# A hybrid trunk layer on one core: memory queries projected earlier, softmax work regrouped between ScalarE and VectorE, mixed scale from a ones matmul

## What is computed

```
h    = RMSNorm(x);  proj = h @ W_in          # q,k,v, gates, pooling input u, memory query q_m
gla  = chunked gated linear attention(q,k,v) , head RMSNorm, * silu(gate)
pool = multi-scale causal mean of u minus u, grouped linear, * silu(gate)
s    = q_m . k_mem / 8                       # 4 heads, 256 memory tokens
p    = softmax(s);  mem = (p . v_mem) * silu(gate)
mixed = concat(gla, pool, mem)
y    = RMSNorm(x + mixed @ W_out)
```

## Time and profile before

| | |
|---|---|
| Median of 3 runs | 1571.4 us (1571.22 to 1571.52) |
| The profiled execution | 1571.57 us, span 1570.1 us |
| TensorE busy | 1442.4 us, 92% of the span |
| VectorE, ScalarE, GpSimd busy | 746.9, 577.3, 334.9 us |
| Chain that ended last | 82% TensorE, 8% VectorE, 3% ScalarE, 2% GpSimd |
| Mean granted TensorE clock | 0.972 of full |

### The profile page before, as it was taken

How to read it: one execution, slowest core, us unless ns; L and a number is a source line. 1 busy time by engine, 2 the same in 40 slices (tenths; PEclk the granted TensorE clock), 3 DMA queues, 4 the chain that set the end, 5 groups by cost and what they waited for, 6 DMA issues and landing times.

```text
span 1570.1 us, 28228 instructions
## 1 busy us (share of the span) xinstructions
PE 1442.4 (92%) x11714; PEld 1042.9 (66%) x11714; DVE 746.9 (48%) x1221; ACT 577.3 (37%) x973; POOL 334.9 (21%) x298
## 2 busy tenths in 40 slices
PE   3259699999999999999999999999999999999985
PEld 2238576766768676776867576676867676676752
DVE  2775626455361726445262635436172645526162
ACT  1344424344342424334242434434242433424231
POOL 1321303031220303122221303122030313122110
PEclk9679799999999999999999999999999999999998
DMA  8130100101020010102010010102001010201001
GB/s 339 56 134 2 41 1 28 54 13 67 0 80 0 27 53 27 53 0 80 0 63 17 27 53 18 62 0 80 0 27 53 27 53 0 80 0 54 1 28 67
DMA packets 15432, 69.32 MB, mean 44 GB/s; under 512 B 2352, under 2 KB 2480, under 8 KB 12848
## 3 DMA queue, kind: packets, MB, share of 16 engines
q1 hardware_dynamic: 15408, 68.98, 11.9%
HBM read 52.20 MB, written 16.78 MB: 44 GB/s over the span
## 4 chain that ended last, share of the span: by engine, by line
PE 82%; DVE 8%; ACT 3%; issue 3%; POOL 2%; DMA 1%; SPq 1%; ACTq 0%; POOLq 0%; DVEq 0%
PE bank L330 69%; PE bank L467 2%; PE bank L475 2%; PE bank L481 2%; PE bank L489 2%; PE bank L532 1%; DVE whl L836 1%; DVE arena L979 1%; DVE nm L988 1%; DVE arena L997 1%; POOL arena L1156 1%; ACT arena L715 1%; PE bank L383 1%; DVE arena L962 1%; DVE mx L985 1%
## 5 line engine op out<-in xcount | busy, mean ns | idle before, releaser
L330 PE MATMUL bank<-arena,whl 128*128 128x256 f16 x6144 | 683.8, 274 | 3.0 <-DVE whl L836 3.0
L330 PEld LDWEIGHTS bank<-arena,whl 128*128 128x128 f16 x6144 | 601.6, 98 | 84.5 <-issue 7.0
L330 PE MATMUL bank<-arena 128*128 128x512 f16 x1536 | 343.5, 381 | 12.3 <-DVE arena L856 12.3
L330 PEld LDWEIGHTS bank<-arena 128*128 128x128 f16 x1536 | 148.2, 98 | 184.8 <-issue 18.6
L947 DVE SCALAR_TENSOR_TENSOR arena<-arena 64x256 f32<-64x256 f32 x60 | 25.2, 420 | 411.9 <-POOL arena L1173 410.5
L330 PE MATMUL bank<-whl,arena 128*128 128x512 f16 x768 | 168.4, 379 | 0.0
L676 ACT ACTIVATE arena<-bank,sca 128x512 f32<-128x512 f32 x64 | 43.9, 687 | 262.8 <-PE bank L330 261.7
L330 PEld LDWEIGHTS bank<-whl,arena 128*128 128x128 f16 x768 | 75.1, 98 | 87.3
L1156 POOL TENSOR_TENSOR arena<-arena 128x512 f16<-128x512 f32 x64 | 89.5, 1410 | 142.3 <-ACT arena L724 142.3
L1166 POOL TENSOR_TENSOR arena<-arena 128x542 f32<-128x542 f32 x16 | 17.3, 1079 | 463.9 <-issue 438.8
L867 DVE SCALAR_TENSOR_TENSOR arena<-bank,sca,arena 128x512 f32<-128x512 f32 x64 | 47.8, 749 | 108.0 <-PE bank L330 91.4
(11 more groups left out here) (154 smaller groups left out, 1516.0 us busy)
## 6 DMA issues: line engine op xcount, KB each, us to landing
arena<-in_xt SPq DMA_DIRECT2D x16, 1024.0 KB, 5.4
arena<-in_x SPq DMA_DIRECT2D x32, 512.0 KB, 3.4
out<-arena SPq DMA_DIRECT2D x32, 512.0 KB, 2.6
arena<-in_w_in SPq DMA_DIRECT2D x8, 768.0 KB, 16.1
arena<-in_w_out SPq DMA_DIRECT2D x1, 4096.0 KB, 12.2
arena<-in_w_in SPq DMA_DIRECT2D x8, 392.0 KB, 16.2
arena<-in_w_mem SPq DMA_DIRECT2D x1, 2048.0 KB, 10.9
arena<-in_memt SPq DMA_DIRECT2D x1, 1024.0 KB, 6.5
```

The costliest lines, as they stand in the source:

```text
L330: mm = nc.tensor.matmul(ap, lhs, rhs, start=k == 0 and n == 0, stop=(k, n) == last)
```

## The change

Five edits, all of them within a pass:

- The memory query is projected second of the four groups, into bank 1; the two gates follow in banks 2 and 3. ScalarE makes the high part of `qst` ahead of the last two gates, and the load of the exponential table now stands behind the last gate.
- VectorE takes the maxima of units 0 and 1 ahead of the masks; the scaled negative maximum `nm` is made by ScalarE.
- `p_norm` is only the reciprocal. The division happens within the split: ScalarE's high part and VectorE's new `p_low` read `pr` and multiply by the reciprocal, head by head (128 x 256 each).
- GpSimd no longer makes the rest of the probabilities.
- The all-reduce is gone: `mix_sum` on TensorE multiplies the per-partition maxima by a matrix of ones into bank 6, behind the keys of the next pass (and at the head of the tail). The scale then comes from the sum of the maxima. GpSimd's carry of S waits for the state and the head outputs.

```diff
+            def mix_sum(n):
+                pe.wait_ge(mmax_ok, n + 4)
+                nc.tensor.matmul(bank[6][:, 0:1], ones[:, :], mmax[:, 1:2], start=True, stop=True).then_inc(m_all, 1)
...
                 features(2, CK).then_inc(pe_k, 1)
+                if not first:
+                    mix_sum(i - 1)
...
-                for n, c in enumerate((CU, CGP, CGM, CQM)):
+                for n, c in enumerate((CU, CQM, CGP, CGM)):
...
-                    if n < 2:
+                    if n == 0:
+                        pe.wait_ge(p2_out, 5 * i + 4)
+                        pe.wait_ge(qm_lo, 2 * (i + 1))
+                    elif n == 1:
                         pe.wait_ge(p2_out, 5 * (i + 1))
-                        pe.wait_ge(qm_lo, 2 * (i + 1))
...
             def tail(n):
+                mix_sum(n - 1)
...
-                silu(4, 1, 4)
-                silu(5, 2, 6)
-                nc.scalar.preload_act_table_set(EXP_LN)
-                act.wait_ge(pe_p2, 6 * i + 6)
+                act.wait_ge(pe_p2, 6 * i + 4)
...
+                silu(5, 2, 4)
+                silu(6, 3, 6)
+                nc.scalar.preload_act_table_set(EXP_LN)
                 act.wait_ge(pe_ket, i + 1)
...
                 def p_exp_of(n):
+                    act.wait_ge(max_ok, 4 * i + n + 1)
+                    nc.scalar.activation(nm[:, 2 * n:2 * n + 2], mx[:, 2 * n:2 * n + 2], ACT.Copy,
+                                         scale=sc_neg).then_inc(nmax_ok, 1)
                     act.wait_ge(nmax_ok, 4 * i + n + 1)
...
-                    nc.scalar.activation(phl[n % 2][:, 0, :, :], pr[n % 2], ACT.Copy).then_inc(p_hi, 1)
+                    for h in range(2):
+                        a = nc.scalar.activation(phl[n % 2][:, 0, h, :], pr[n % 2][:, h, :], ACT.Copy,
+                                                 scale=rsum[:, 2 * n + h:2 * n + h + 1])
+                    a.then_inc(p_hi, 1)
...
-                nc.vector.tensor_scalar(m_tmp, mmax[:, 2:3], TINY, None, ALU.max).then_inc(m_tiny, 1)
+                nc.vector.tensor_scalar(m_tmp, bank[6][:, 0:1], TINY, None, ALU.max).then_inc(m_tiny, 1)
...
-                    r = rsum[:, 2 * n:2 * n + 2].unsqueeze(2).broadcast_to([P, 2, NMEM])
-                    nc.vector.tensor_tensor(pr[n % 2], pr[n % 2], r, ALU.mult).then_inc(pn_ok, 1)
+                def p_low(n):
+                    dve.wait_ge(p_hi, 4 * i + n + 1)
+                    for h in range(2):
+                        a = nc.vector.scalar_tensor_tensor(phl[n % 2][:, 1, h, :], pr[n % 2][:, h, :],
+                                                           rsum[:, 2 * n + h:2 * n + h + 1], phl[n % 2][:, 0, h, :],
+                                                           ALU.mult, ALU.subtract)
+                    a.then_inc(p_lo, 1)
...
-                for n in range(4):
-                    p_lo_of(i, n)
...
-                nc.gpsimd.partition_all_reduce(mmax[:, 2:3], mmax[:, 1:2], P, RMAX).then_inc(m_all, 1)
```

More of the change, by code:

```diff
@@ L692, in step @@
                     r = slice(64 * h, 64 * h + 64)
-                    nc.scalar.activation(qst[r, :, h, :], bank[3][r, :].rearrange("p (a t) -> p a t", a=2), ACT.Copy,
+                    nc.scalar.activation(qst[r, :, h, :], bank[1][r, :].rearrange("p (a t) -> p a t", a=2), ACT.Copy,
                                          scale=2.0 ** -QBITS).then_inc(qm_hi, 1)
+                silu(5, 2, 4)
+                silu(6, 3, 6)
+                nc.scalar.preload_act_table_set(EXP_LN)
                 act.wait_ge(pe_ket, i + 1)
@@ L720, in p_hi_of @@
                 def p_hi_of(n):
-                    act.wait_ge(pn_ok, 4 * i + n + 1)
+                    act.wait_ge(rs_ok, 4 * i + n + 1)
                     if n >= 2:
                         act.wait_ge(pe_pt, 4 * i + n - 1)
-                    nc.scalar.activation(phl[n % 2][:, 0, :, :], pr[n % 2], ACT.Copy).then_inc(p_hi, 1)
+                    for h in range(2):
+                        a = nc.scalar.activation(phl[n % 2][:, 0, h, :], pr[n % 2][:, h, :], ACT.Copy,
+                                                 scale=rsum[:, 2 * n + h:2 * n + h + 1])
+                    a.then_inc(p_hi, 1)
                 p_exp_of(0)
@@ L961, in step @@
                     dve.wait_ge(qm_hi, 2 * i + h + 1)
-                    nc.vector.scalar_tensor_tensor(qst[other, :, h, :], bank[3][r, :].rearrange("p (a t) -> p a t", a=2),
+                    nc.vector.scalar_tensor_tensor(qst[other, :, h, :], bank[1][r, :].rearrange("p (a t) -> p a t", a=2),
                                                    2.0 ** -QBITS, qst[r, :, h, :], ALU.mult,
@@ L986, in mem_max @@
                                             AX.X, ALU.max).then_inc(max_ok, 1)
-                    dve.wait_ge(max_ok, 4 * i + n + 1)
-                    nc.vector.tensor_scalar(nm[:, 2 * n:2 * n + 2], mx[:, 2 * n:2 * n + 2], sc_neg, None,
-                                            ALU.mult).then_inc(nmax_ok, 1)
                 def p_norm(n):
@@ L994, in p_norm @@
                     nc.vector.reciprocal(rsum[:, 2 * n:2 * n + 2], psum_p[:, 2 * n:2 * n + 2]).then_inc(rs_ok, 1)
-                    dve.wait_ge(rs_ok, 4 * i + n + 1)
-                    r = rsum[:, 2 * n:2 * n + 2].unsqueeze(2).broadcast_to([P, 2, NMEM])
-                    nc.vector.tensor_tensor(pr[n % 2], pr[n % 2], r, ALU.mult).then_inc(pn_ok, 1)
+                def p_low(n):
[5 more added lines that the diff above has]
+                    a.then_inc(p_lo, 1)
                 def state(c):
@@ L1032, in rows @@
                         add_rows(i - 1, n)
+                mem_max(0)
+                mem_max(1)
                 masked(0)
                 masked(1)
-                mem_max(0)
-                mem_max(1)
                 p_norm(0)
                 p_norm(1)
+                p_low(0)
+                p_low(1)
                 rows(0)
@@ L1047, in step @@
                 p_norm(3)
+                p_low(2)
                 rows(1)
@@ L1050, in step @@
                 pt_copy(1, 7)
+                p_low(3)
                 state(3)
@@ L1152, in _ @@
             nc.gpsimd.memset(S[:, 0, :, :], 0.0).then_inc(s_carry, 1)
-            def p_lo_of(i, n):
-                pool.wait_ge(p_hi, 4 * i + n + 1)
-                nc.gpsimd.tensor_tensor(phl[n % 2][:, 1, :, :], pr[n % 2], phl[n % 2][:, 0, :, :],
-                                        ALU.subtract).then_inc(p_lo, 1)
             def step(i, first, last):
@@ L1176, in step @@
                     fold_rows(sq, 3 * (i + 1), sq_add)
-                for n in range(4):
-                    p_lo_of(i, n)
                 if not last:
                     x_lo_of(i + 1)
-                if not first:
-                    pool.wait_ge(m_sc, i)
-                pool.wait_ge(mmax_ok, i + 4)
-                nc.gpsimd.tensor_tensor(idle[:, 2:3], eps[:, 0:1], eps[:, 1:2], ALU.add)
                 if not last:
+                    pool.wait_ge(pe_o, 2 * (i + 1))
+                    pool.wait_ge(s_ok, 4 * (i + 1))
+                    nc.gpsimd.tensor_tensor(idle[:, 2:3], eps[:, 0:1], eps[:, 1:2], ALU.add)
                     nc.gpsimd.tensor_copy(S[:, 0, :, :], S[:, NC, :, :]).then_inc(s_carry, 1)
-                nc.gpsimd.partition_all_reduce(mmax[:, 2:3], mmax[:, 1:2], P, RMAX).then_inc(m_all, 1)
             run_blocks(pool, step, lambda n: None)
```

## The result

The changed kernel takes 1580.8 us (median of 4 runs, 1580.6 to 1582.0) against 1571.5 for the kernel before in the same stretch of runs: 9.3 us or 0.6% longer, ratio 1.0060, 95% interval 1.0042 to 1.0077. The forecast was 1576.3. The direction was right, and the measured time lies inside the stated range, but the forecast rise was 4.4 us too small.

A forecast was written before the change was run, and what follows sets the result against it. TensorE, busy 92%, was taken to bound the kernel. 14 loop passes x (0.4 + 0.22) = +8.7, first pass +1.0, last 0, tail -4.8 gave +4.9 on 1571.4: 1576.3 us, range 1566 to 1584.

The forecast's parts named there:

- `quarter(0)`: Its start on TensorE in a loop pass, behind gate, table load and `ket`: 869.1 instead of 869.36, about 0.25 us gained.
- the rival of the table load: Rival: ScalarE's table load costs more with work right behind it, up to 1.1 us; +21, 1592 us; chance 0.05.
- Squares and exponentials: ScalarE in a loop pass: squares end at 870.66 instead of 869.94, exponentials of unit 0 start at 871.0 against 872.56.
- `p_low`: VectorE's rest of a unit: two instructions of 0.42 us, some 0.8 us, against 1.28 on GpSimd.
- The meeting with GpSimd: `p_low(0)` on VectorE meets GpSimd's last addition: 0.38 us lost, 0.2 taken as reaching the end of `p_low(1)`.
- Handover to `add_rows`: VectorE behind `p_low(1)`: `add_rows` starts at 876.25, not 875.81; maximum of unit 2 at 878.1, not 877.69.
- `turn_p(2)`: TensorE waits 1.2 us there in each loop pass and is 0.4 us later per pass, range +0.15 to +0.6.
- `mix_sum`: The ones matmul on TensorE behind the keys costs 0.22 us per pass, between 0 and 0.44.
- First pass: No quarter of the output projection covers the lengthened chain there: +1.0 us, range 0 to 1.5.
- Tail: End of the kernel, without the all-reduce: `mixed_hi` at 1530.5 and all behind it 4.8 us earlier, once.
- the last rival: Rival: the tail gives less since TensorE's clock falls in the gap anyway; 1 us or so, no chance of its own.
- GpSimd holds `p_low` fully: Rival: the whole collision loss arrives in the loop and `mix_sum` costs 0.35: +9.8, 1581 us; chance 0.15.

The follow-up runs named there:

- e4: The changed kernel with GpSimd's third addition of the squares held until unit 1's rest is written: 1574.3 us, ratio 1.0019, pass 90.02 us.
- e7: The changed kernel with the masks ahead of the maxima again on VectorE: 1579.3 us in one run, pass 90.38 us.
- e1: The kernel before with only the ones matmul in place of the all-reduce: 1568.9 us, ratio 0.9984, pass 89.65 us.
- e5: The changed kernel with the next block's squares moved between ScalarE's last two gates: 1557.4 us, ratio 0.9907, pass 88.81 us.
- e2: The kernel before with only the query projected second and the table load behind the last gate: 1574.2 us, ratio 1.0017, pass 89.65 us.

## Why the prediction was right in direction and too small

Step by step, in times within the pass:

- **`quarter(0)`**: forecast 3.07 (869.1), measured 3.04. Gate, load and `ket` follow each other as worked out: the load ends at 875.12, and `ket` starts at 875.14. With that the rival of the table load falls; it needed up to 1.1 us there. The Trainium skill, "ScalarE: Activation LUTs", section "What ACT_TABLE_LOAD costs", gives a drain of about 1380 ns beside the load of 1283; here the load takes 1.28 us, and no drain shows behind it or between the gate and it (873.84 follows a gate that began at 873.14).
- **Squares and exponentials**: squares end at 4.60 (forecast 4.63), exponentials from 4.94 (4.97), unit 1's high part at 9.16 (9.32). Right; the high part takes 0.498 us (0.51 forecast) and `nm` 0.288 (0.29).
- **`p_low`**: 0.48 us alone (0.42 forecast, from a row of 64 partitions and fp32), and yet its end without the meeting, 8.40 + 1.68 = 10.08 (as in e4), is close to the forecast one (10.12).
- **The meeting with GpSimd is the term that was mis-sized.** The prediction had 0.38 lost once and took 0.2 of it, for the rest of unit 1 would catch a part. e4 measured 0.47, and all of it reached the end of `p_low(1)`: 10.54. The Trainium skill's rule in "SBUF — State Buffer", "Who interferes with whom", that a VectorE instruction with two SBUF inputs and a reading GpSimd instruction exclude each other, agrees with this trace: the second `p_low` of unit 0 ends 0.3 us behind the addition and takes 0.95 instead of 0.48. The sum of 0.6 per pass that the prediction drew from it was the nearer one.
- **Handover to `add_rows`**: forecast 0.1 before the end of `p_low(1)`, measured 0.03 behind it (in e7 0.07 before it). Another 0.13. The maximum of unit 2 is at 12.46 (forecast 12.07). From there to `turn_p(2)` it is 5.52 (5.50 forecast).
- **`turn_p(2)`**: 17.98 against 17.57, so 0.84 per pass later than before and not 0.4; of the missing 0.41 us the meeting is 0.27 and the handover 0.13.
- **`mix_sum`**: 0.14 in e1 and in the changed kernel, not 0.22.
- **First pass**: forecast +1.0, measured 0.0 by the second pass's transpose. The chain did get longer: `turn_p(2)` starts 17.18 us behind the first transpose (151.96 to 169.14), before 16.38 (152.58 to 168.96). Two things cover the 0.80. The first transpose is 0.62 earlier, and that need not be the change: the kernel before and e1 have the same program up to there and differ by 0.9 (152.58, 153.50). And TensorE works at a granted clock of 0.50 until 174.26, before until 174.91, which gives back 0.3. So p.v starts at 176.72, before at 176.90. The prediction had neither; no run isolates them.
- **Tail**: forecast -4.8, measured -4.9 at TensorE's restart and -4.6 at the end. The granted clock takes the rest, as the last rival had it. It is low until about 1553.2, 4.4 us behind the restart, instead of 3.8 us. After, two windows (us, busy, granted clock of full, DMA share, GB/s):

```profile
1548.80:1552.00 3.20, 3.20 (x8) 0.50 0.46 164
...
1553.00:1554.00 1.00, 1.00 (x6) 0.88 0.00 0
```

and before, which stood still longer ahead of it:

```profile
1539.86:1543.66 3.80, 3.80 (x10) 0.50 0.40 138
1543.66:1544.66 1.00, 1.00 (x6) 1.00 0.00 0
```

0.50 is the level of 1.2 GHz and 1.00 that of 2.4. The 0.6 us more at the low level account for 0.3.

In sum: 14 passes +13.9 where 8.7 were forecast, the first pass 1.0 less, the tail 0.2 more: 4.4 us in all. The mechanism was right, one wait at `turn_p(2)` in place of two earlier ones, and its signs came, with 1.5 us at `turn_p(2)` for 1.2 and 0.98 a pass for 0.6. That the sum was not further off was luck: `turn_p(2)` alone was 6 us short in 14 passes, and `mix_sum` (1.1 too dear) and the first pass (1.0 that did not arrive) hid a third of it. Of the rivals it came nearest to "GpSimd holds `p_low` fully" (+9.8), but with another division: it too had `turn_p(2)` short (0.6 of 0.84), `mix_sum` too dear (0.35), and a first pass that did not arrive (+1.3).

What the prediction missed altogether is what e5 shows. It saw that `nm(0)` must wait in ScalarE's queue for the squares, and it weighed whether the chain would be late, but took the place of the squares, and with it that of GpSimd's additions, as given. It also read L988 only as a line that leaves VectorE's queue, and never looked at its duration; there stood 1.31 and 0.72 us for an instruction of 0.23, the first sign of how much GpSimd's additions weigh on VectorE here.

## What to carry to other kernels

When a wait of the bounding engine is taken away, follow each queue of the chain behind it: here 1.2 us in front of one piece came out as 1.5 us in front of another, and moving 1.9 us of unrelated work from ahead of the chain on ScalarE took the new wait away (e5). Work that has slack (squares whose sum TensorE takes up only behind `quarter(2)`) belongs in a hole of its engine, and a wait belongs in front of the instruction that reads the data. Look at the first pass too, where the same move can meet other work: in e5 it cost up to 2.6 us there. Where one engine's tiny instruction takes several times its usual time, look at what GpSimd does at that moment, before moving more work to VectorE near it.

## What the runs showed of the hardware

- Of VectorE's instructions in this kernel, `nm` (128 x 2, with a scale from SBUF) took 2.11 us beside GpSimd's addition, where it takes 0.23 alone (e2), and a 64 x 16 instruction of the pooling means 2.32 instead of 0.17 (e5). The size of the instruction does not protect it.
- Two `p_low` that stand back to back do not keep GpSimd out. In the changed kernel the first instruction of unit 0 ran from 8.40 to 8.88 within the pass, GpSimd's third addition from 8.45 to 9.47, and the second `p_low` from 8.80 to 9.75: 0.95 us instead of 0.48, and 1.02 for the addition instead of 0.73. The addition ended between the two, and both sides lost.
- The ones matmul for one column costs 0.14 us in the stream of a pass (e1), and in the tail 0.52 us from its start to the first VectorE instruction behind it (1542.03 to 1542.55). From the end of the maximum to `mixed_hi` it is 2.30 us (1541.98 to 1544.28) with it, the last 1.0 of them behind the scale, for ScalarE's norm step; it was 7.26 with the all-reduce (1528.07 to 1535.33).
